# Scores of the last attention in three products of rounded parts, with two head groups on 64 rows each

## The chip, the cores and the metric

One core of a Trainium2 chip runs the whole program as one launch. The metric is the device time in microseconds. The clock of TensorE has two levels here, 1.2 and 2.4 GHz; the profile gives the granted clock of a stretch as a share of the upper one.

## The reference

Two model blocks over 512 tokens of width 1024, all in fp32. The first block has windowed attention with 12 heads, a retention branch and an MLP. The second has a short convolution layer and then an attention layer with three branches (`nsa_attention`): 16 query heads of width 64, 4 key and value groups. With 512 tokens and blocks of 64, all eight key blocks are selected, so the selected branch is a causal attention over all keys, and the window branch, window 512, is the same with other keys and values:

```
s_s = einsum(qr, kg) * scale;  p_s = masked_softmax(s_s);  o_s = p_s @ vg
s_w = einsum(qr, kw) * scale;  p_w = masked_softmax(s_w);  o_w = p_w @ vw
return g[..., 0:1] * o_c + g[..., 1:2] * o_s + g[..., 2:3] * o_w
```

The output of the attention is multiplied by silu(z), goes through one more projection, and the sum with the residual is normalized.

## The kernel before

Five engine programs are written from one list, `ORDER` (made by `make_order`). Each engine goes through this list and does its share of every token, strictly in the order of the list; semaphores carry the dependencies. `make_order` places tokens by tables of positions: `KV` for the projection stage of the last attention (a position is a step of TensorE's products), and for the attention itself one round per score unit, with `FILL` saying how many steps of other products (gate tiles `nz` 4 to 7, then the output projection `bo`) stand at three places of each round. The tables are written out as numbers in the file.

Almost all products are of the "rounded high and low" kind: an operand x is kept as a rounded copy h (type fp32r, ScalarE) and the remainder l = x - h (VectorE), and a product is h*h + h*l + l*h. This is how `mm` (L909), the retention (L998, L1009) and the values (L1141) work. The scores of the last attention (`scores_n`, L1115) are plain fp32 products instead.

The queries lie in `nqr[p]` (p is one of two pairs of key groups): partitions 0 to 63 are one group, 64 to 127 the other, each with four heads i. The keys lie in `ksT[:, n, p]` in the same way, n being the branch. There are 44 units `UNITS[u] = (p, qb, n, i0, cnt)`: a query block qb of 128 rows against N = (qb + 1) * 128 keys, for cnt heads in each of the two groups f. A unit takes two banks of a ring of three, one per f. The two groups' products read different 64 rows of the array. A bf16 product (L1118) adds the causal mask. Then, per unit: VectorE takes the maximum (L2140), ScalarE the exponential with its sum (L1161), GpSimd scales (L2230), TensorE turns the probabilities three rounds later (L1129, `LAG` = 3), ScalarE copies them rounded (L1536), VectorE takes the remainder (L2157), and TensorE makes the values (L1141). When a query block is complete, `gather` adds the halves (L1544, L2166), `gate_o` multiplies by silu(z) (L2178) and `split_o` makes high and low parts (L1560, L2184).

In the projection stage before it, keys and queries are projected and rotated (`rope_k`, `rope_q`, VectorE L2072, L2085), the compressed branch is computed (`cmp_scores`, `cmp_turn`, VectorE L2098 to L2126, ScalarE L1507), and weights are split (L1177 on ScalarE, L1636 on VectorE). Its last tokens are four `silu` on ScalarE; the first exponentials wait for the end of this stage on all engines.

Of the kernel before, what the change touches and what calls it, by code (L numbers as in the profile page):

```python
# [7 lines left out]
F32 = mybir.dt.float32  # L8
# [6 lines left out]
S = 512  # L15
# [294 lines left out]
def make_order():  # L310
# [83 lines left out]
    def some(n):  # L394
# [9 lines left out]
            out.append(pieces.pop(0))  # L404
        return out

    for r in range(len(UNITS) + LAG + 1):
        for G in GROUPS:
            if GROUPS[G][-1] == r - LAG - 1:
                if G == FIRST_GROUP[G[0], G[1]]:  # L410
                    o.append(("cmp_values", G[0], G[1]))
                o.append(("values_n", *G))
                if G == LAST_GROUP[G[0], G[1]]:
                    o.append(("gather", G[0], G[1]))
        o += some(FILL[r][0])
        if 0 <= r - LAG < len(UNITS):
            o.append(("turn_n", r - LAG))
        if 0 <= r - 1 < len(UNITS):
            o.append(("rate", r - 1))
        o += some(FILL[r][1])  # L420
        if r < len(UNITS):
            o.append(("scores_n", r))
        o += some(FILL[r][2])
        if r == SILU_AT:
            o += [("silu", f) for f in range(4, 8)]
        for G in GATED_AT:
            if GATED_AT[G] == r:
# [7 lines left out]
    for b in range(4):  # L435
# [4 lines left out]

LAG = 3

KV = {"k": 21, "v": 30, "gates": 23, "silu": 122, ("rope", 0, 0): 23, ("cmp", 0, 0): 43,
      ("turn", 0, 0): 64, ("rope", 0, 1): 36, ("cmp", 0, 1): 45, ("turn", 0, 1): 69, ("rope", 0, 2): 37,
      ("cmp", 0, 2): 52, ("turn", 0, 2): 75, ("rope", 0, 3): 41, ("cmp", 0, 3): 59, ("turn", 0, 3): 79,
      ("rope", 1, 0): 57, ("cmp", 1, 0): 82, ("turn", 1, 0): 95, ("rope", 1, 1): 67, ("cmp", 1, 1): 83,
# [10 lines left out]
SILU_AT = 22  # L457
GATED_AT = {(0, 0): 22, (0, 1): 24, (0, 2): 28, (0, 3): 38, (1, 0): 27, (1, 1): 32, (1, 2): 39}
ATT = {("norm", "q", 0, 0): 30, ("turn", "q", 0, 0): 51, ("norm", "q", 0, 1): 33, ("turn", "q", 0, 1): 54,
# [163 lines left out]
def program(nc, ctx, a, out):  # L623
# [77 lines left out]
        rs2 = sb("rs2", [128, S], F32, ph)  # L701
    ph3 = ExitStack()
    oT = sb("oT", [128, 8, S], F32, ph3)
    nqr = [sb(f"nqr{p}", [128, 4, S], F32, ph3) for p in range(2)]
    with ExitStack() as ph:
        nqu = [sb(f"nqu{p}", [128, 4, S], F32, ph) for p in range(2)]
    pcs = [sb(f"pc{p}", [128, 4, S], F32R, ph3) for p in range(2)]
    with ExitStack() as ph:
        cb = sb("cb", [128, 256], BF16, ph)
        cm = sb("cm", [128, 160], F32, ph)  # L710
        kcT = sb("kcT", [128, 2, 64], F32, ph)
        vc = sb("vc", [128, 4, 128], F32R, ph)
        ksT = sb("ksT", [128, 2, 2, S], F32, ph)
        v2 = sb("v2", [128, 4, 8, 128], F32R, ph)
        zx = sb("zx", [128, 2, S], F32, ph)
# [31 lines left out]
    Fb = [t[:, :, :].rearrange("p (a b) (c d) -> p a b c d", a=2, c=2) for t in (nqu[1], nqr[1])]  # L747

    XS = {"x": (xh, xl, "xl"), "or": (orh, orl, "orl"), "oa": (oah, oal, "oal"), "y": (yh, yl, "yl"),
          "h": (hh, hl, "hl"), "cy": (cyh, cyl, "cyl"), "z": (xh, xl, "zl")}  # L750
# [56 lines left out]
        return sl[(p * 4 + qb) % 2]  # L807

    def z_slot(f):
        return oT[:, 4 + f, :] if f < 4 else zx[:, f - 4, :] if f < 6 else tmp45[:, f - 6, :]  # L810

    def xo(b, c=None):

# [15 lines left out]
    def split_views(name, r, hi, lo):  # L829
# [20 lines left out]
    def tensor(e):  # L850
# [253 lines left out]
        def scores_n(u):  # L1104
            p, qb, n, i0, cnt = UNITS[u]
            qs = slice(qb * 128, qb * 128 + 128)
            N = (qb + 1) * 128
            two = [take("scores_n", ("scores_n", u, f), ("exp_n", u, f)) for f in range(2)]
            w.wait_ge(*told("cab"))
            w.wait_ge(*told("rope_done", "k", n, p))  # L1110
            for j in range(cnt):
                w.wait_ge(*told("rope_done", "q", p, i0 + j))
                for f, bank in enumerate(two):
                    hf = slice(64 * f, 64 * f + 64)
                    e.matmul(bank[:, j * N:(j + 1) * N], nqr[p][hf, i0 + j, qs], ksT[hf, n, p, 0:N], start=True,  # L1115
                             stop=False)
                for f, bank in enumerate(two):
                    m = e.matmul(bank[:, (j + 1) * N - 128:(j + 1) * N], idb, cab, start=False, stop=True)  # L1118
                    if j == cnt - 1:
                        m.then_inc(*tell("scores_n", u, f))  # L1120
# [33 lines left out]
    def scalar(e):  # L1154
# [348 lines left out]
        def cmp_turn(p, qb):  # L1503
# [78 lines left out]
        def end(phase):  # L1582
            S_.close(phase, "act")
            if phase == "att":
# [2 lines left out]

        follow(w_, w_part, w_piece, x_norm, x_in, x_raw, square, root, norm, v, rv, q, k_, norm_qk, turn_qk, scores, probs, values, mix_log, mix_pick, rq, rk,
               decay_parts, next_decay, rg, ret, gated_ret, ga, pb, split_oa, gb, pa, wo, up, down, z, ao, nsa_consts, fold, vsw, gate,
               hidden, compressed_v, nq_, cmp_scores, cmp_turn, scores_n, turn_n, gather, nz, silu, split_o,  # L1590
               final_gain, x_out, bo, bo_end, end)


    def vector(e):
# [413 lines left out]
        def key_in(n, p):  # L2008
# [15 lines left out]
        def rope_k(n, p):  # L2024
# [11 lines left out]
            e.tensor_tensor(ksT[:, n, p, :], ksT[:, n, p, :], t[:, :], ALU.add).then_inc(*tell("rope_done", "k", n, p))  # L2036

        def hidden(n):
            e.memset(hid[n][:, :, :, :, 31:32], 0.0).then_inc(*tell("hid_end", n))
# [29 lines left out]
        def nq_(p, i):  # L2069
            w.wait_ge(*told("out_a", ("nq", p, i)))  # L2070
            w.wait_ge(*told("cn"))
            e.tensor_tensor(nqr[p][:, i, :], nqu[p][:, i, :], cos, ALU.mult).then_inc(*tell("rope_cos", "q", p, i))  # L2072

        def rope_q(p, i):
            t = tmp[4 + p]
# [9 lines left out]
            e.tensor_tensor(nqr[p][:, i, :], nqr[p][:, i, :], t[:, :], ALU.add).then_inc(*tell("rope_done", "q", p, i))  # L2085

        def cmp_scores(p, qb):
            n = CMP.index((p, qb))
# [83 lines left out]
        def gate_o(p, qb):  # L2172
            c = slice(qb * 128, qb * 128 + 128)
            w.wait_ge(*told("silu", 4 * p + 3))
            w.wait_ge(*told("gathered", p, qb, 1))
            for k, z in ((4, zx), (6, tmp45)) if p else ((0, oT),):
                n = 2 if p else 4
                m = e.tensor_tensor(oT[:, k:k + n, c], oT[:, k:k + n, c], z[:, 0 if p else 4:2 if p else 8, c], ALU.mult)  # L2178
            m.then_inc(*tell("silu_mul", p, qb))

        def split_o(p, qb):
# [26 lines left out]
        def end(phase):  # L2208
# [1 line left out]

        follow(x_in, w_part, w_piece, x_norm, square, w_, root, norm, q, k_, norm_qk, turn_qk, scores, mix_log, mix_pick, mix, rq, rk, rv, decay, decay_parts, ret, gated_ret, pb, split_oa,
               gb, pa, wo, down, ao, up, c_, u, b_, z, nsa_consts, ck, cv, turn_rs, ks, kw, rope_k, hidden, compressed_k,
               compressed_v, gates, nq_, rope_q, vsw, cmp_scores, cmp_turn, scores_n, rate, turn_n, gather, gate_o,
               split_o, bo, bo_gain, bo_end, end)


# [133 lines left out]
```

## Time and profile before

| | us |
|---|---|
| median of three runs | 2043.85 |
| the three runs | 2041.2 to 2047.33 |
| span of the profiled execution | 2042.4 |
| projection stage of the last attention, from about | 1700 to 1795 |
| its attention rounds | 1795 to 2012 |

The page gives TensorE 98% of the span, VectorE 51%, ScalarE 38%, GpSimd 4%. The profile gives the time of its execution only as the span. In the rows below, PE is TensorE, PEld its weight loads, DVE VectorE, ACT ScalarE, POOL GpSimd. A busy time of PE covers the latency of a product too, so that products overlap in it; the distance of two starts is the pace.

### The profile page before, as it was taken

How to read it: one execution, taken by the hardware profiler on the slowest of the kernel's cores; microseconds unless marked ns; L12 is line 12 of the kernel's file. 1: busy time of each engine (PE TensorE's matmuls, PEld its weight loads, DVE VectorE, ACT ScalarE, POOL GpSimd, SP SyncE). 2: the span in 40 equal slices, each digit the busy share in tenths (PEclk: the TensorE clock that was granted, in tenths of full speed). 3: DMA queues.
4: the chain of work that ended last, by engine and by line, in shares of the span. 5: the costliest groups of instructions: out<-in, count | busy, mean ns of one | idle time of the engine just before them, and what ended most of it. 6: DMA issues, size and time to landing. Idle time of an engine off the chain costs nothing.

```text
span 2042.4 us, 22755 instructions
## 1 busy us (share of the span) xinstructions
PE 1996.0 (98%) x9502; PEld 1651.3 (81%) x9502; DVE 1051.4 (51%) x1415; ACT 771.5 (38%) x1232; POOL 80.6 (4%) x132
## 2 busy tenths in 40 slices
PE   7999999999999999999999999999999999999898
PEld 6899987888888888888888888888888788866566
DVE  4444447545454346643244455455454465856675
ACT  4554563342324323342143222212222214366764
POOL 0000000000000000000000000000000000033431
PEclk9999999999999999999999999999999999999999
DMA  5121222223232232233323332332333345210002
GB/s 206 63 83 62 83 83 67 88 88 97 74 103 66 100 103 83 91 97 102 103 89 97 103 100 86 103 103 83 103 103 83 119 124 152 80 42 22 32 21 63
DMA packets 186502, 181.25 MB, mean 89 GB/s; under 512 B 4896, under 2 KB 162976, under 8 KB 186400
## 3 DMA queue, kind: packets, MB, share of 16 engines
q1 hardware_dynamic: 182912, 172.41, 27.5%
q10 hardware_dynamic: 3488, 7.38, 1.3%
q8 instruction: 75, 1.23, 0.3%
q14 instruction: 27, 0.22, 0.0%
HBM read 173.49 MB, written 4.19 MB: 87 GB/s over the span
## 4 chain that ended last, share of the span: by engine, by line
PE 82%; DVE 9%; ACT 6%; issue 2%; DMA 1%; ACTq 0%; SPq 0%; DVEq 0%
PE bank L909 75%; ACT tmp L1161 2%; DVE tl L2157 2%; PE bank L1009 1%; DVE rs L2140 1%; ACT wh L1177 1%; PE bank L998 1%; ACT raw L1161 1%; PE bank L1141 1%; DVE wl L1636 1%; PE bank L1115 1%; DVE oT L2166 1%; ACT th L1536 0%; PE bank L919 0%; ACT pb L1161 0%
## 5 line engine op out<-in xcount | busy, mean ns | idle before, releaser
L909 PE MATMUL bank<-xh,wh 128*128 128x512 f32 x1352 | 534.7, 395 | 1.7 <-DVE wl L1636 1.1
L909 PE MATMUL bank<-xh,wl 128*128 128x512 f32 x1352 | 527.3, 390 | 0.0
L909 PE MATMUL bank<-xl,wh 128*128 128x512 f32 x1352 | 526.9, 390 | 0.0
L1636 DVE TENSOR_TENSOR wl<-raw,wh 128x2048 fp32r<-128x2048 f32 (+2 forms) x154 | 342.3, 2225 | 267.8 <-ACT wh L1177 267.5
L1177 ACT CAST wh<-raw 128x2048 fp32r<-128x2048 f32 (+2 forms) x154 | 285.2, 1854 | 382.3 <-PE bank L909 370.3
L909 PEld LDWEIGHTS bank<-xh,wh 128*128 128x128 f32 x1352 | 253.6, 188 | 55.4 <-issue 3.2
L909 PEld LDWEIGHTS bank<-xh,wl 128*128 128x128 f32 x1352 | 253.3, 187 | 54.2
L909 PEld LDWEIGHTS bank<-xl,wh 128*128 128x128 f32 x1352 | 253.7, 188 | 51.0 <-issue 0.7
L909 PE MATMUL bank<-wh,xh 128*128 128x512 f32 x512 | 213.5, 417 | 4.7 <-DVE xl L2184 4.0
L909 PE MATMUL bank<-wl,xh 128*128 128x512 f32 x512 | 202.0, 395 | 0.0
L909 PE MATMUL bank<-wh,xl 128*128 128x512 f32 x512 | 202.0, 395 | 0.0
L909 PEld LDWEIGHTS bank<-wh,xh 128*128 128x128 f32 x512 | 120.3, 235 | 17.1 <-issue 4.4
L909 PEld LDWEIGHTS bank<-wh,xl 128*128 128x128 f32 x512 | 120.1, 235 | 13.0
L909 PEld LDWEIGHTS bank<-wl,xh 128*128 128x128 f32 x512 | 121.2, 237 | 10.8
L2230 POOL TENSOR_SCALAR tmp<-tmp,rs 128x128 f32<-128x128 f32 (+3 forms) x88 | 54.4, 632 | 1884.7 <-DVE rs L2148 1884.7
L1161 ACT ACTIVATE tmp<-tmp 128x512 f32<-128x512 f32 (+2 forms) x61 | 36.6, 603 | 193.6 <-DVE tmp L1598 100.6
L909 PE MATMUL bank<-hh,wh 128*128 128x512 f32 x256 | 99.6, 389 | 0.0
L909 PE MATMUL bank<-hl,wh 128*128 128x512 f32 x256 | 99.6, 389 | 0.0
L909 PE MATMUL bank<-hh,wl 128*128 128x512 f32 x256 | 99.6, 389 | 0.0
L1885 DVE TENSOR_TENSOR xT<-xT,bank 128x512 f32<-128x512 f32 x32 | 22.0, 686 | 122.4 <-PE bank L909 122.4
L2157 DVE TENSOR_TENSOR tl<-bank,th 128x512 fp32r<-128x512 f32 (+1 forms) x88 | 52.4, 637 | 42.4 <-ACT th L1536 42.1
L1401 ACT CAST xh<-tmp 128x512 fp32r<-128x512 f32 x24 | 14.9, 621 | 150.0 <-DVE tmp L1894 150.0
(270 smaller groups left out, 2597.8 us busy)
## 6 DMA issues: line engine op xcount, KB each, us to landing
raw<-in_w_in SPq DMA_DIRECT2D x49, 1024.0 KB, 5.1
raw<-in_a_w_in SPq DMA_DIRECT2D x32, 1024.0 KB, 5.7
raw<-in_w_up SPq DMA_DIRECT2D x16, 1024.0 KB, 5.4
raw<-in_w_down SPq DMA_DIRECT2D x16, 1024.0 KB, 5.7
raw<-in_w_proj_b SPq DMA_DIRECT2D x8, 1024.0 KB, 5.1
raw<-in_a_w_out SPq DMA_DIRECT2D x8, 1024.0 KB, 5.6
raw<-in_w_out SPq DMA_DIRECT2D x4, 1024.0 KB, 5.0
raw<-in_w_kv SPq DMA_DIRECT2D x4, 1024.0 KB, 4.9
```

What stands on the lines that cost most here:

```text
L909: m = e.matmul(o, p, q, start=k == 0 and n == 0, stop=k == K - 1 and n == 2)
L998: m = e.matmul(bank[:, 0:n], k[:, kb * 128:(kb + 1) * 128], q[:, kb * 128:], start=j == 0 and x == 0, stop=j == 1 and x == 2)
L1009: m = e.matmul(bank[:, :], r[:, (qb - kb) * 128:(qb - kb + 1) * 128], v[:, kb, :], start=kb == 0 and x == 0, stop=kb == qb and x == 2)
L1115: e.matmul(bank[:, j * N:(j + 1) * N], nqr[p][hf, i0 + j, qs], ksT[hf, n, p, 0:N], start=True, stop=False)
L1141: m = e.matmul(bank_of("acc", (p, qb, f))[:, i0 * 128:(i0 + cnt) * 128], v2[:, k, n * 4 + p * 2 + f, :], t[:, 0:cnt * (qb + 1) * 128].rear ...
L1161: return e.activation(o, i, f, scale=scale, **kw)
L1177: m = e.copy(hi, r)
L1636: m = e.tensor_tensor(lo, r, hi, ALU.subtract)
L1885: e.tensor_tensor(xT[:, k, :], xT[:, k, :], tile_bank(key)[:, :], ALU.add).then_inc(*tell("out_d", key))
L2140: e.tensor_reduce(wt[:, c:c + cnt], bank_of("scores_n", ("scores_n", u, f))[:, 0:cnt * N].rearrange("p (s k) -> p s k", s=cnt), AX, ALU.ma ...
L2157: e.tensor_tensor(lo[:, o:o + m], bank_of("turn_n", ("turn_n", u, f))[:, 0:m], hi[:, o:o + m], ALU.subtract).then_inc(*tell("lo_n", u, f))
L2230: m = e.tensor_scalar(x, x, wt[:, 32 + c + j:33 + c + j], gts[:, qb, (p * 2 + f) * 4 + i0 + j, 1 + n:2 + n], ALU.mult, ALU.mult)
```

## The change

Queries and keys are first written in fp32 to `nqf` and `ksf` (the memory of `nqr` and `ksT`), and are then split: the rounded part by ScalarE, the remainder by VectorE, in place. Eight tokens `split_q` (512 columns each) and two `split_k` (1024 columns each) do this. `split_k` 0 stands at step 60 and `split_q` (0, 0) at the end of the projection stage, the others at the start of the rounds 0, 4, 12, 20, 22, 26, 34, and `split_k` 1 in round 20. `scores_n` makes three products for each head and group. To make room, the gate tiles 4 to 7 go to other memory, and wait for what was there.

```
+    extra += [(KV["split_k"], ("split_k", 0)), (KV["split_q"], ("split_q", 0, 0))]
...
+    splits = {r: [("split_q", p, qb)] for (p, qb), r in SPLIT_Q_AT.items()}
+    splits[SPLIT_K_AT].insert(0, ("split_k", 1))
     for r in range(len(UNITS) + LAG + 1):
+        o += splits.get(r, [])
...
+SPLIT_Q_AT = {(0, 1): 0, (0, 2): 4, (0, 3): 12, (1, 0): 20, (1, 1): 22, (1, 2): 26, (1, 3): 34}
+SPLIT_K_AT = 20
...
     def z_slot(f):
-        return oT[:, 4 + f, :] if f < 4 else zx[:, f - 4, :] if f < 6 else tmp45[:, f - 6, :]
+        return oT[:, 4 + f, :] if f < 4 else tmp45[:, 5 - f, :] if f < 6 else pcf[:, f - 6, :]
...
+            w.wait_ge(*told("split_lo", "k", p))
+            w.wait_ge(*told("split_lo", "q", p, qb))
+            qh, ql, kh, kl = q_hi(p, qb), nqr[p][:, :, qs], k_hi(p), ksT[:, :, p, :]
             for j in range(cnt):
-                w.wait_ge(*told("rope_done", "q", p, i0 + j))
-                for f, bank in enumerate(two):
-                    hf = slice(64 * f, 64 * f + 64)
-                    e.matmul(bank[:, j * N:(j + 1) * N], nqr[p][hf, i0 + j, qs], ksT[hf, n, p, 0:N], start=True,
-                             stop=False)
+                for x, (q, k) in enumerate(((qh, kh), (qh, kl), (ql, kh))):
+                    for f, bank in enumerate(two):
+                        hf = slice(64 * f, 64 * f + 64)
+                        e.matmul(bank[:, j * N:(j + 1) * N], q[hf, i0 + j, :], k[hf, n, 0:N], start=x == 0, stop=False)
...
+        def split_k(p):                     # ScalarE
+            w.wait_ge(*told("rope_done", "k", 1, p))
+            if p:
+                w.wait_ge(*told("cmp_pv", 0, 3))
+            else:
+                after("conv")
+            e.copy(k_hi(p), ksf[:, :, p, :]).then_inc(*tell("split_hi", "k", p))
+
+        def split_q(p, qb):                 # ScalarE
+            w.wait_ge(*told("rope_done", "q", p, 3))
+            if q_hi_before(p, qb):
+                w.wait_ge(*told("scores_n", LAST_UNIT[q_hi_before(p, qb)], 1))
+            elif qb:
+                w.wait_ge(*told("rope_done", "q", 1, 3))
+            e.copy(q_hi(p, qb), nqf[p][:, :, qb * 128:qb * 128 + 128]).then_inc(*tell("split_hi", "q", p, qb))
...
             after("kv" if f >= 4 else "conv")
+            if f == 5:
+                w.wait_ge(*told("scores_n", LAST_UNIT[0, 0], 1))
+            elif f > 5:
+                w.wait_ge(*told("cmp_pv", 0, f - 6))
...
+        def split_k(p):                     # VectorE
+            w.wait_ge(*told("split_hi", "k", p))
+            e.tensor_tensor(ksT[:, :, p, :], ksf[:, :, p, :], k_hi(p), ALU.subtract).then_inc(*tell("split_lo", "k", p))
+
+        def split_q(p, qb):                 # VectorE
+            c = slice(qb * 128, qb * 128 + 128)
+            w.wait_ge(*told("split_hi", "q", p, qb))
+            e.tensor_tensor(nqr[p][:, :, c], nqf[p][:, :, c], q_hi(p, qb), ALU.subtract).then_inc(*tell("split_lo", "q", p, qb))
...
-            for k, z in ((4, zx), (6, tmp45)) if p else ((0, oT),):
-                n = 2 if p else 4
+            for k, z in ((4, tmp45[:, 1:2, c]), (5, tmp45[:, 0:1, c]), (6, pcf[:, 0:2, c])) if p else ((0, oT[:, 4:8, c]),):
+                n = z.shape[1]
```

## Rows read from the trace of the kernel before

**Rows 1.** Busy us (and instructions) of each engine in two stretches, granted clock, DMA.
```profile
1742.00:1797.00 55.00, 53.30 (x285) 43.62 (x284) 47.15 (x99) 21.47 (x32) 0.00 (x0) 1.00 0.27 81
1795.00:2012.00 217.00, 197.63 (x1212) 138.43 (x1212) 138.06 (x283) 142.00 (x401) 80.39 (x128) 0.97 0.08 25
```
**Rows 2.** Chain of waits, 1876 to 1893 us: start, us, what.
```profile
1878.49 0.60 DVE rs L2140
1879.11 1.45 ACT tmp L1161 x4
1880.56 0.55 ACT th L1536
1881.13 1.29 DVE tl L2157 x2
...
1882.49 0.60 DVE rs L2140
```
**Rows 3.** Chain of waits from 1780 us on: shares by line, then pieces.
```profile
by line: DVE tl L2157 14.1%; ACT tmp L1161 12.6%; PE bank L909 11.1%; DVE rs L2140 7.8%; ACT raw L1161 5.7%; PE bank L1141 5.6%; PE bank L1115 5.4%; DVE oT L2166 4.7%; issue 4.7%; ACT th L1536 3.9%; PE bank L1129 2.9%; DVE xl L2184 1.9%; DM
...
1959.63 1.43 PE bank L1141 x12
...
1962.41 0.85 PE bank L1115 x4
...
1988.91 1.06 PE bank L1115 x4
```
**Rows 4.** Timeline of PE: start, us, instruction, count; score and mask products.
```profile
1795.14 0.49 PE L1115 MATMUL bank<-ksT,nqr 64*128 64x128 f32 x4
1795.56 0.28 PE L1118 MATMUL bank<-cb 128*128 128x128 bf16 x2
...
1941.03 0.59 PE L1115 MATMUL bank<-ksT,nqr 64*128 64x384 f32 x2
...
1941.45 0.49 PE L1115 MATMUL bank<-ksT,nqr 64*128 64x384 f32 x2
...
1941.87 0.28 PE L1118 MATMUL bank<-cb 128*128 128x128 bf16 x2
```
**Rows 5.** Timeline of PEld in the same unit: its second two loads.
```profile
1941.13 0.19 PEld L1115 LDWEIGHTS bank<-ksT,nqr 64*128 64x128 f32 x2
```
**Rows 6.** Timeline of PE: rounded products of the retention, 512 and 128 columns.
```profile
337.96 1.52 PE L998 MATMUL bank<-rqk 128*128 128x512 f32 x6
...
347.97 0.78 PE L998 MATMUL bank<-rqk 128*128 128x128 f32 x6
```
**Rows 7.** Timeline of ACT and DVE: two weight splits of 1024 columns.
```profile
1736.07 1.99 ACT L1177 CAST wh<-raw 128x1024 fp32r<-128x1024 f32 x2
...
1738.09 2.36 DVE L1636 TENSOR_TENSOR wl<-raw,wh 128x1024 fp32r<-128x1024 f32 x2 [1.20 <-ACT wh L1177]
```
**Rows 8.** Single lines: count, min/median/max ns, first and last start.
```profile
L1560 ACT CAST xh<-oT x8: 601/620/629, 1904.1 to 2014.3; 128x512 fp32r<-128x512 f32 x8
...
L2184 DVE TENSOR_TENSOR xl<-oT,xh x8: 692/692/820, 1904.8 to 2014.9; 128x512 fp32r<-128x512 f32 x8
```
**Rows 9.** Timeline of ACT, PE and DVE around the first scores; [idle before <-releaser].
```profile
1783.31 0.42 ACT L1161 ACTIVATE tmp<-tmp 128x256 f32<-128x256 f32 x1 [2.84 <-DVE tmp L2103]
...
1792.36 0.63 PE L1093 MATMUL bank<-base,tmp 128*64 128x128 f32 x4 [1.13 <-DVE pc L2126]
...
1796.02 2.19 ACT L1161 ACTIVATE oT<-oT 128x512 f32<-128x512 f32 x4
...
1796.58 0.69 DVE L2126 TENSOR_TENSOR pc<-bank,pc 64x512 fp32r<-64x512 f32 x1
...
1799.57 0.37 ACT L1161 ACTIVATE tmp<-bank,rs 128x128 f32<-128x128 f32 x1
```
**Rows 10.** Stretch as in rows 1, after the second score unit.
```profile
1806.20:1812.90 6.70, 6.70 (x27) 4.30 (x27) 2.10 (x4) 4.67 (x19) 3.57 (x9) 0.50 0.00 0
```
**Rows 11.** Timeline of PE: the scores of the third unit.
```profile
1806.16 1.22 PE L1115 MATMUL bank<-ksT,nqr 64*128 64x256 f32 x4 [1.61 <-ACT tmp L1161]
```

More of the change, by code:

```diff
@@ L441 @@
 LAG = 3
-KV = {"k": 21, "v": 30, "gates": 23, "silu": 122, ("rope", 0, 0): 23, ("cmp", 0, 0): 43,
+KV = {"split_k": 60, "split_q": 110, "k": 21, "v": 30, "gates": 23, "silu": 122, ("rope", 0, 0): 23, ("cmp", 0, 0): 43,
       ("turn", 0, 0): 64, ("rope", 0, 1): 36, ("cmp", 0, 1): 45, ("turn", 0, 1): 69, ("rope", 0, 2): 37,
@@ L703, in program @@
     oT = sb("oT", [128, 8, S], F32, ph3)
-    nqr = [sb(f"nqr{p}", [128, 4, S], F32, ph3) for p in range(2)]
+    with ExitStack() as ph:
+        nqf = [sb(f"nqf{p}", [128, 4, S], F32, ph) for p in range(2)]
+    nqr = [sb(f"nqr{p}", [128, 4, S], F32R, ph3) for p in range(2)]
     with ExitStack() as ph:
         nqu = [sb(f"nqu{p}", [128, 4, S], F32, ph) for p in range(2)]
+    with ExitStack() as ph:
+        pcf = sb("pcf", [128, 4, S], F32, ph)
     pcs = [sb(f"pc{p}", [128, 4, S], F32R, ph3) for p in range(2)]
@@ L712, in program @@
         vc = sb("vc", [128, 4, 128], F32R, ph)
-        ksT = sb("ksT", [128, 2, 2, S], F32, ph)
+        with ExitStack() as ph2:
+            ksf = sb("ksf", [128, 2, 2, S], F32, ph2)
+        ksT = sb("ksT", [128, 2, 2, S], F32R, ph)
         v2 = sb("v2", [128, 4, 8, 128], F32R, ph)
-        zx = sb("zx", [128, 2, S], F32, ph)
+        kh0 = sb("kh0", [128, 2, S], F32R, ph)
         with ExitStack() as ph2:
@@ L746, in program @@
     Ab = nqu[0][:, :, :].rearrange("p (a b) (c d) -> p a b c d", a=2, c=2)
-    Fb = [t[:, :, :].rearrange("p (a b) (c d) -> p a b c d", a=2, c=2) for t in (nqu[1], nqr[1])]
+    Fb = [t[:, :, :].rearrange("p (a b) (c d) -> p a b c d", a=2, c=2) for t in (nqu[1], nqf[1])]
     XS = {"x": (xh, xl, "xl"), "or": (orh, orl, "orl"), "oa": (oah, oal, "oal"), "y": (yh, yl, "yl"),
@@ L809, in z_slot, with q_hi, q_hi_before, k_hi @@
     def z_slot(f):
-        return oT[:, 4 + f, :] if f < 4 else zx[:, f - 4, :] if f < 6 else tmp45[:, f - 6, :]
+        return oT[:, 4 + f, :] if f < 4 else tmp45[:, 5 - f, :] if f < 6 else pcf[:, f - 6, :]
+    def q_hi(p, qb):
+        if (p, qb) == (0, 0):
+            return rsl1[:, 0, :].rearrange("p (i q) -> p i q", i=4)
+        if (p, qb) == (0, 1):
+            return th2[:, S:2 * S].rearrange("p (i q) -> p i q", i=4)
+        if qb >= 2:
+            return nqr[p][:, :, (qb - 2) * 128:(qb - 1) * 128]
+        return nqr[0][:, :, 0:128] if qb else nqr[0][:, :, 256:384]
+    def q_hi_before(p, qb):
+        return {(0, 2): (0, 0), (0, 3): (0, 1), (1, 0): (0, 2), (1, 1): (0, 2), (1, 2): (1, 0), (1, 3): (1, 1)}.get((p, qb))
+    def k_hi(p):
+        return pcs[0][:, 2:4, :] if p else kh0[:, :, :]
     def xo(b, c=None):
@@ L837, in split_views @@
         return [(r, hi, lo)]
+    LAST_UNIT = {(x[0], x[1]): u for u, x in enumerate(UNITS)}
     LAST_P0 = max(u for u, x in enumerate(UNITS) if x[0] == 0)
@@ L1109, in scores_n @@
             w.wait_ge(*told("cab"))
-            w.wait_ge(*told("rope_done", "k", n, p))
+            w.wait_ge(*told("split_lo", "k", p))
+            w.wait_ge(*told("split_lo", "q", p, qb))
+            qh, ql, kh, kl = q_hi(p, qb), nqr[p][:, :, qs], k_hi(p), ksT[:, :, p, :]
             for j in range(cnt):
-                w.wait_ge(*told("rope_done", "q", p, i0 + j))
-                for f, bank in enumerate(two):
-                    hf = slice(64 * f, 64 * f + 64)
-                    e.matmul(bank[:, j * N:(j + 1) * N], nqr[p][hf, i0 + j, qs], ksT[hf, n, p, 0:N], start=True,
-                             stop=False)
+                for x, (q, k) in enumerate(((qh, kh), (qh, kl), (ql, kh))):
+                    for f, bank in enumerate(two):
+                        hf = slice(64 * f, 64 * f + 64)
+                        e.matmul(bank[:, j * N:(j + 1) * N], q[hf, i0 + j, :], k[hf, n, 0:N], start=x == 0, stop=False)
                 for f, bank in enumerate(two):
@@ L1589, in scalar @@
                decay_parts, next_decay, rg, ret, gated_ret, ga, pb, split_oa, gb, pa, wo, up, down, z, ao, nsa_consts, fold, vsw, gate,
-               hidden, compressed_v, nq_, cmp_scores, cmp_turn, scores_n, turn_n, gather, nz, silu, split_o,
+               hidden, compressed_v, nq_, cmp_scores, cmp_turn, split_k, split_q, scores_n, turn_n, gather, nz, silu, split_o,
                final_gain, x_out, bo, bo_end, end)
@@ L2015, in key_in @@
             w.wait_ge(*told("cn"))
-            e.tensor_tensor(ksT[:, n, p, :], t[:, :], cos, ALU.mult).then_inc(*tell("rope_cos", "k", n, p))
+            e.tensor_tensor(ksf[:, n, p, :], t[:, :], cos, ALU.mult).then_inc(*tell("rope_cos", "k", n, p))
         def ks(p):
@@ L2035, in rope_k @@
             w.wait_ge(*told("rope_cos", "k", n, p))
-            e.tensor_tensor(ksT[:, n, p, :], ksT[:, n, p, :], t[:, :], ALU.add).then_inc(*tell("rope_done", "k", n, p))
+            e.tensor_tensor(ksf[:, n, p, :], ksf[:, n, p, :], t[:, :], ALU.add).then_inc(*tell("rope_done", "k", n, p))
         def hidden(n):
@@ L2071, in nq_ @@
             w.wait_ge(*told("cn"))
-            e.tensor_tensor(nqr[p][:, i, :], nqu[p][:, i, :], cos, ALU.mult).then_inc(*tell("rope_cos", "q", p, i))
+            e.tensor_tensor(nqf[p][:, i, :], nqu[p][:, i, :], cos, ALU.mult).then_inc(*tell("rope_cos", "q", p, i))
         def rope_q(p, i):
@@ L2084, in rope_q @@
             w.wait_ge(*told("rope_cos", "q", p, i))
-            e.tensor_tensor(nqr[p][:, i, :], nqr[p][:, i, :], t[:, :], ALU.add).then_inc(*tell("rope_done", "q", p, i))
+            e.tensor_tensor(nqf[p][:, i, :], nqf[p][:, i, :], t[:, :], ALU.add).then_inc(*tell("rope_done", "q", p, i))
         def cmp_scores(p, qb):
@@ L2175, in gate_o @@
             w.wait_ge(*told("gathered", p, qb, 1))
-            for k, z in ((4, zx), (6, tmp45)) if p else ((0, oT),):
-                n = 2 if p else 4
-                m = e.tensor_tensor(oT[:, k:k + n, c], oT[:, k:k + n, c], z[:, 0 if p else 4:2 if p else 8, c], ALU.mult)
+            for k, z in ((4, tmp45[:, 1:2, c]), (5, tmp45[:, 0:1, c]), (6, pcf[:, 0:2, c])) if p else ((0, oT[:, 4:8, c]),):
+                n = z.shape[1]
+                m = e.tensor_tensor(oT[:, k:k + n, c], oT[:, k:k + n, c], z, ALU.mult)
             m.then_inc(*tell("silu_mul", p, qb))
@@ L2212, in vector @@
                gb, pa, wo, down, ao, up, c_, u, b_, z, nsa_consts, ck, cv, turn_rs, ks, kw, rope_k, hidden, compressed_k,
-               compressed_v, gates, nq_, rope_q, vsw, cmp_scores, cmp_turn, scores_n, rate, turn_n, gather, gate_o,
+               compressed_v, gates, nq_, rope_q, vsw, cmp_scores, cmp_turn, split_k, split_q, scores_n, rate, turn_n, gather, gate_o,
                split_o, bo, bo_gain, bo_end, end)
```

## The prediction

> **What bounds the kernel now.** I read the page's busy times first, then the stretches, then the chain of waits, then single instructions. The page gives TensorE 98% of the span, which says nothing about the last attention alone. The stretches do: from 1795 to 2012 us TensorE is busy 197.6 of 217 us, VectorE 138.1, ScalarE 142.0 [rows 1]. So nobody is full, and a wait must be found. The chain of waits shows two kinds of bound. In most rounds it never touches TensorE: the maximum of a score tile (VectorE L2140, 0.60), two exponentials (ScalarE L1161, 1.45), the first rounded copy of an older turned tile (ScalarE L1536, 0.55), two remainders of it (VectorE L2157, 1.29), a reciprocal, and the next maximum, 4.00 us later [rows 2]. Each engine works its list in order, so VectorE and ScalarE wait for each other in a ring, and TensorE fits beside it. In other rounds filler products and score products are on the chain: L1141, L909, and then the scores of round 35 at 1962.41 [rows 3]. The reader should see that these are different resources: a shorter score product helps only in the second kind, and one more instruction on ScalarE or VectorE hurts in the first.
>
> **What the score products cost now.** One head pair (j) with 384 keys: two matmuls start together at 1941.03, one for each half of the rows; the next two at 1941.45; the mask product at 1941.87 [rows 4]. The second loads are issued at 1941.13 [rows 5]. I read this as 0.105 us for a load that nothing covers, two passes of 0.32 us over 384 columns (2 cycles a column at 2.4 GHz), and 0.10 us until the mask product. The same formula gives 0.42 for 128 columns (rows: 1795.14 to 1795.56), 0.845 for 384 (0.85), and 1.06 for 512 (1.06) [rows 3, 4], so 0.635 for 256 is safe. The pairs therefore already overlap in fp32; that the heads sit on 64 rows each is not new.
>
> **What they cost after.** Three rounded passes instead of two fp32 passes. A rounded pass is one column a cycle: six products of 512 columns take 1.52 with a last one of 0.389, so 0.226 apart [rows 6]; twelve of 256 columns take 1.43, 0.119 apart [rows 3]; I put 384 between at 0.175. For 128 columns the six take 0.78 with a last one of about 0.22, so 0.112 apart [rows 6]: the weight load sets the pace there, not the 0.053 of streaming. No row shows two rounded products on 64 rows each side by side; I take it that they overlap as the fp32 ones do. For one j:
> - 128 columns: 0.105 + 2 x 0.112 + 0.055 + 0.10 = 0.49, against 0.42: 0.07 more
> - 256: 0.105 + 3 x 0.119 + 0.10 = 0.56, against 0.635: 0.07 less
> - 384: 0.73, against 0.845: 0.11 less
> - 512: 0.885, against 1.06: 0.175 less
>
> There are 16 j of each size, so TensorE is given back 16 x 0.285 = 4.6 us. If no pair overlapped the passes would double, and a j would take 0.83, 0.92, 1.26, 1.56: 26 us more. The bounds are -4.6 and +26; I take the first, since the same two half arrays overlap in the rows. All j together take 16 x (0.42 + 0.635 + 0.85 + 1.06) = 47 us now, and the chain from 1780 us to the end (262 us) has 5.4% on L1115, 14 us [rows 3]; so I count 14 x 4.6 / 47, -1.4, on the path.
>
> Here a rule bears on the sum. The pairs start 0.42 apart in two fp32 passes and each pass is fully shared [rows 4]. The Trainium skill (TensorE: Matmul & The Clock Gate, Part 3: Packing small matmuls) states that products on different row groups run side by side, but gives 3.07 times for four of them. By that factor a shared pass would be 1.3 times as long, a j of 512 columns an estimated 1.09 instead of 0.885, and the 4.6 us would be gone. Nothing else below uses this.
>
> **What is added.** Eight copies of a 128x512 piece of the queries (ScalarE) and eight subtractions (VectorE), two each of 128x1024 for the keys. Nearest rows: 1.99 for two and 2.36 for two of 128x1024, so 1.0 and 1.18 [rows 7]; 0.62 and 0.69 for 128x512 [rows 8]. By order:
> - split_k(0), step 60 of the projection stage. VectorE is busy 47.2 of 55 us there [rows 1], and its idle gaps are waits for a ScalarE exponential that itself had waited 2.84 us for VectorE [rows 9]. So the two go in lockstep from about 1758 on. TensorE waits at the end for VectorE: 1.13 us at 1792.36 [rows 9]. The 1.0 of the copy runs beside; the 1.18 of the subtraction moves the end. +1.2.
> - split_q(0,0) at the last step and split_q(0,1) at the start of round 0. ScalarE runs four Silu from 1796.02, a table load, and the first exponential at 1799.57 [rows 9], with no gap between. Two copies go in. VectorE ends the projection stage with the remainder at 1796.58 [rows 9], and now has two subtractions before the first maximum; the second waits for its copy, behind the Silu. And the first score product waits for split_q(0,0): 1797.27 + 1.2 + 0.69 = 1799.15 instead of 1795.14. Four j of 0.49 and three masks of 0.22 end at 1801.8, the maximum takes 0.6, so the first exponential starts at 1802.7: +3.1, of which +1.2 is the line above. +1.9. The second score unit is again 128 columns: +0.2 (its four j lie on the path).
> - Rounds 4, 12, 26: one split_q each, between the exponentials of one round and the rounded copy of the next. ScalarE gives up 0.5 to 0.6, then subtraction (0.62 from start to start) and L1536 (0.55) run side by side. +0.67 each, +2.0. All three rounds are ring rounds like [rows 2].
> - Round 20: split_k(1) and split_q(1,0). Copy 1.0, then subtraction 1.15 and subtraction 0.62 against 0.55 of L1536 that they cover: +2.2. This is the ring of [rows 2] itself.
> - Round 22: before four Silu and two table loads on ScalarE: +0.65.
> - Round 34: the copy delays a ring in a TensorE stretch; round 35's scores wait for TensorE until 1962.41 [rows 3], and the delayed exponential would be ready at 1961.7. Nothing, or 0.67 if that cover goes.
> - gate_o for the second half: three multiplications instead of two, +0.05 to +0.1 each: +0.2. The gate tiles' new slots add waits for the scores of unit 1 and for cmp_values, both long done when nz 5, 6 and 7 land: nothing. The SP queue and its transfers are not moved.
>
> Every other new wait looks two rounds ahead (a block's pieces are split two rounds before its first scores) and costs nothing; behind the first score product 12 filler products are queued, and they had 3 us of slack.
>
> **The sum.** 1.2 + 1.9 + 0.2 + 2.0 + 2.2 + 0.65 + 0.2 - 1.4 = +7.0 us. The profile gives its execution by the span of 2042.4 alone; that is 1.4 under the median of 2043.85 and inside the three runs (2041.2 to 2047.33). Profiled span after: 2049.4; on the median: 2050.8. Each added piece counts 0 if TensorE covers it and its full copy plus subtraction if nothing overlaps, so the additions lie between 1.9 and 14.
>
> **Rivals.**
> - A, TensorE is the engine that decides (91% busy in the stage): the additions of the rounds fall in the 75 us that ScalarE is idle, and all 4.6 are on the path. For it: the stretches of [rows 3]. Against: the ring of [rows 2], with TensorE waiting at every second round. 1.2 + 1.9 - 4.6 = -1.5; if the half-speed stretch from 1806 to 1813 (granted clock 0.50 [rows 10]) goes too, about -4: 2040 to 2042. It decides as soon as ScalarE and VectorE have over 0.7 us spare in the rounds named.
> - B, half the additions are hidden and the gain on the path is 2.5: +2.5, 2046.5.
> - C, the clock. TensorE now idles 3 us before the first scores. In the profile the stretch at the lower level, 1.2 GHz [rows 10], begins with an idle time of 1.61 us before 1806.16 [rows 11]. If it comes at once, the four j take twice as long, +2.6, and the later one may stay: 2053.5.
> - D, rounded pairs do not overlap: +26 us of TensorE against 19 us of idle time in the stage, of which about half can take it up: 2043.85 + 3 + 15 = 2062.
>
> **How the numbers follow.** My forecast (+7.0) 0.42, A 0.12, B 0.22, C 0.16, D 0.08. The range must take in B and C and half of A: 2043 to 2057. A measurement of this kernel tells about 0.3% (6.1 us) from no change: faster means under 2037.7, slower over 2050.0. The forecast lies just beyond that edge: of it 0.55 is slower, with C and D, so 0.47; faster needs more than A and gets 0.06; the rest, 0.47, is within.
>
> **What would show it.** A j of 512 columns from first score to mask 0.88 (if 1.06 or more, the pass rule is wrong; if 1.5, D). Pairs of matmuls 6 ns apart, three times. First scores at 1799 and first exponential at 1802.7. The maximum of round 20 about 2.2 us later against that of round 19 than now (4.0 between them), TensorE idle in it. Distance from the first maximum of round 34 to that of 35 shorter by 0.6. If the distance between rounds 4, 12 and 26 and those before does not grow, the ring is not what bounds, and A is right.

## The result, and the profile after

| | before | after |
|---|---|---|
| median us (4 runs each) | 2043.09 | 2057.22 |
| lowest to highest | 2041.2 to 2047.33 | 2054.96 to 2058.73 |
| span of the profiled execution | 2042.4 | 2054.5 |

The ratio is 1.0067, 95% interval 1.0056 to 1.0079: slower by 0.67%, and clear of noise, since the interval lies well above 1. The forecast was 2050.8, range 2043 to 2057: right in direction, too small by 6.4 us, and the time lies 0.2 us above the range. The two spans differ by 12.1 us, and the rest of this section accounts for those.

The busy times of the same two stretches (columns as in [rows 1]) seem to say the opposite of the result. In the second, TensorE is busy 188.0 us instead of 197.6, VectorE and ScalarE about as long as before. But the rounds now end 12 us later, so that the same 217 us hold less of their work: the figures don't mean that TensorE was given back 10 us.

```profile
1742.00:1797.00 55.00, 52.24 (x263) 42.53 (x261) 47.16 (x99) 21.76 (x32) 0.00 (x0) 0.97 0.26 80
1795.00:2012.00 217.00, 188.01 (x1274) 141.64 (x1274) 137.66 (x283) 140.20 (x396) 76.45 (x125) 0.96 0.07 23
```

**The score products.** Timeline of PE in the changed kernel, one j of 512 columns (start, us, instruction, count). From the first score product to the mask it takes 0.89 us.

```profile
1989.23 0.50 PE L1147 MATMUL bank<-pc,nqr 64*128 64x512 f32 x2
1989.57 0.39 PE L1147 MATMUL bank<-ksT,nqr 64*128 64x512 f32 x2
1989.80 0.39 PE L1147 MATMUL bank<-pc,nqr 64*128 64x512 f32 x2
1990.12 0.28 PE L1149 MATMUL bank<-cb 128*128 128x128 bf16 x2
```

The reader should see "x2" three times: the two head groups start together, and the third pair follows the second by 0.23, one pass of 512 columns. Over all rounds the median j takes 0.48, 0.56, 0.73 and 0.89 for the four sizes, forecast 0.49, 0.56, 0.73 and 0.885. In the kernel before the medians were 0.42, 0.635, 0.85 and 1.06, so TensorE is given back 5.0 us (forecast 4.6). Shared passes are not longer than single ones here. The Trainium skill (TensorE: Matmul & The Clock Gate, Part 3: Packing small matmuls) gives 3.07 times for four products; the prediction's estimate from it, passes 1.3 times as long, is not seen for two.

**The start.** Timelines of PE, DVE and ACT around the first unit; in brackets the idle time before, and what ended it.

```profile
1797.87 0.69 DVE L2187 TENSOR_TENSOR nqr<-nqf,rsl 128x512 fp32r<-128x512 f32 x1
...
1798.71 0.33 PE L1147 MATMUL bank<-kh,rsl 64*128 64x128 f32 x2 [1.65 <-DVE nqr L2187]
...
1801.97 1.29 DVE L2200 TENSOR_REDUCE rs<-bank 128x4 f32<-128x512 f32 x2 [1.43 <-PE bank L1149]
...
1802.69 0.37 ACT L1192 ACTIVATE tmp<-bank,rs 128x128 f32<-128x128 f32 x1 [1.58 <-DVE rs L2200]
```

TensorE waits for the remainder of block (0, 0) and starts at 1798.71 (forecast 1799.15); the first exponential starts at 1802.69 (forecast 1802.7), 3.1 us after that of [rows 9]. This execution was already 0.52 us ahead of that of before at 1688, ahead of everything that was changed; so the delay that the change makes is 3.6 us, not the 3.1 of the forecast. `split_k` 0 is 1.1 of it (forecast 1.2): the first maximum of the compressed scores behind it (L2101, then L2152) is at 1775.99 instead of 1775.41, in a list that ran 0.52 ahead.

**Round 20.** Chain of waits of the changed kernel: start, us, what. This is the ring of [rows 2] with two splits in it.

```profile
1886.94 0.60 DVE rs L2200
1887.54 0.03 issue
1887.57 1.45 ACT tmp L1192 x4
1889.01 0.94 ACT pc L1546
1889.96 0.03 issue
1889.98 1.23 DVE ksT L2182
1891.21 0.60 DVE nqr L2187
1891.81 0.61 DVE tl L2217
1892.42 0.04 issue
1892.47 3.40 PE bank L1172 x16
```

The copy L1546 and the subtractions L2182 and L2187 add 0.94 + 1.23 + 0.60; the rounded copy (0.55) that stood there in [rows 2] has gone under them: 2.2. What follows was not forecast: the 16 value products take 3.40, 0.21 apart, because the clock is down.

**The clock.** Six stretches of the changed kernel (columns as in [rows 1]; the granted clock is the third number from the end).

```profile
1793.98:1797.39 3.41, 2.93 (x6) 1.82 (x6) 2.62 (x3) 3.38 (x5) 0.00 (x0) 0.50 0.00 0
1800.80:1804.21 3.41, 3.41 (x16) 2.81 (x15) 1.29 (x2) 1.83 (x10) 0.00 (x0) 0.50 0.24 90
1892.96:1896.37 3.41, 3.41 (x19) 3.41 (x18) 1.30 (x4) 1.45 (x4) 1.52 (x2) 0.50 0.00 0
1995.37:1998.77 3.40, 3.40 (x17) 3.40 (x18) 1.68 (x4) 1.45 (x4) 1.52 (x2) 0.50 0.51 154
...
1789.98:1793.40 3.42, 1.23 (x8) 0.65 (x6) 2.77 (x8) 3.21 (x7) 0.00 (x0) 1.00 0.91 304
1806.20:1812.90 6.70, 5.14 (x51) 3.50 (x49) 1.29 (x2) 2.77 (x17) 3.19 (x8) 1.00 0.00 0
```

In the first four TensorE is granted 0.50 (1.2 GHz) while it has work. Before the first of them it was busy 1.23 of 3.42 us; before the third it idled 2.80 us, until 1892.47. The last line is the stretch of [rows 10], which ran at 0.50 in the kernel before and runs at 1.00 here. The clock is also at 0.50 from 1913.44 to 1920.27, where the account below shows no loss; the kernel before has two such stretches, from 1905.13 and from 1929.02.

**The whole account.** For each round I take the start of its first maximum (L2140 before, L2200 after) and subtract: a ladder of shifts, whose steps show where time arises. They add up to the spans' difference.

| step | forecast | measured |
|---|---|---|
| projection stage, first unit, second unit | +3.3 | +3.56, then +2.07 in round 1, then -2.17 in rounds 2 and 3, where the slow stretch of before is absent: +3.46 |
| rounds 4, 12, 26 | +2.0 | 0.60 + 0.74 + 0.64 = +1.98 |
| round 20 | +2.2 | +2.20 |
| round 21 | 0 | +1.55 (clock 0.50) |
| round 22 | +0.65 | +0.60 |
| rounds 24, 25 (gate_o) | +0.2 | +0.33 |
| rounds 34, 35 | 0 | +0.74, -0.30: +0.44 |
| round 41 | 0 | +1.36 (clock 0.50) |
| TensorE's gain | -1.4 | 0.10 + 0.11 + 0.17 + 0.18: -0.56 |
| after the last round, and rest | 0 | +0.71 |
| sum | +7.0 | +12.07 |

The -2.17 in the first line is not the change's doing. A kernel with the scores and splits of before (slots alone, below) was profiled at a span of 2039.7 us, 2.7 under that of before, and it wins the same in rounds 2 and 3, -1.22 and -0.75: its clock doesn't fall there (columns as in [rows 1], now of that kernel).

```profile
1806.20:1812.90 6.70, 6.67 (x44) 4.31 (x44) 3.97 (x8) 4.42 (x18) 4.45 (x10) 1.00 0.00 0
```

So the profiled execution of before happened to hold a slow stretch worth about 2 us. The start costs 5.6 us rather than 3.46, and that is about what the ladder's 12.1 lacks against the 14.1 of the medians.

### The profile page after: what moved, and what is told of

The parts are those of the page before. It is cut to its first block, busy times and chain, and to the rows that moved or that the text cites. A ratio compares the mean times of both kernels' runs of the same rounds, so it can differ in the third digit from the quotient of the medians.

```text
span 2054.5 us, 23037 instructions
## 1 busy us (share of the span) xinstructions
PE 1995.4 (97%) x9630; PEld 1662.5 (81%) x9630; DVE 1058.2 (52%) x1429; ACT 777.0 (38%) x1242; POOL 79.9 (4%) x132
## 4 chain that ended last, share of the span: by engine, by line
PE 81%; DVE 10%; ACT 6%; issue 2%; DMA 1%; ACTq 0%; SPq 0%; DVEq 0%
PE bank L939 73%; ACT tmp L1192 2%; DVE tl L2217 2%; PE bank L1039 1%; DVE wl L1687 1%; ACT wh L1208 1%; DVE rs L2200 1%; PE bank L1172 1%; PE bank L1028 1%; ACT raw L1192 1%; DVE oT L2226 1%; PE bank L1147 1%; PE bank L949 0%; PE bank L1160 0%; ACT pb L1192 0%
```

## Experiments

My theory: ScalarE and VectorE, one after the other, set the time of most rounds, so that each split costs what it adds to this ring, and the score products' time hardly counts. Rivals: TensorE decides; the new slots cost something; the lower clock carries most of it. Shifts below are against the profiled execution of before. Up to 1688 us, where nothing is changed, profiled executions differ by -1.45 to +0.54 us; small ends of the ladders carry this. Medians are given beside those of the kernel before on the same chip.

### The parts one at a time

**Splits without the products.** All splits are done, and the scores stay fp32.

```
-                for x, (q, k) in enumerate(((qh, kh), (qh, kl), (ql, kh))):
+                for f, bank in enumerate(two):
+                    e.matmul(bank[...], nqf[p][hf, i0 + j, qs], ksf[hf, n, p, 0:N], start=True, stop=False)
```

> The scores stay plain fp32 products, as before, but all ten splits (ScalarE copy, VectorE subtraction) are done where the change puts them, their results unused, and the gate tiles are in their new slots. Theory (the splits lie in the ring of ScalarE and VectorE): nearly all of the change's loss is here, +3 at the first scores, +0.6 to 0.75 at each of the rounds 4, 12, 22, 26, +2.2 at round 20; with stretches at the lower clock 9 to 13 us over the kernel before. Rival 1 (the loss is TensorE's: three passes, six weight loads, a lower clock from their shortness): at most +4. Rival 2 (the gate tiles' slots and waits): as much as the change, and the slots alone as well.

Measured: 2056.22 against 2042.18, ratio 1.0066 (1.0052 to 1.0079): the whole loss. The first maximum is at +4.83, more than the 3 I expected, and round 1 adds +2.93 (clock 0.50 from 1801.1 to 1807.9). The steps are +0.60 in round 4, +0.74 in 12, +2.19 in 20, +2.15 in 21 (clock 0.50 from 1893.2 to 1900.1), +0.60 in 22, +0.63 in 26.

**Products without the splits.** Three products of the same rounded operands; the low parts are left out.

```
-                for x, (q, k) in enumerate(((qh, kh), (qh, kl), (ql, kh))):
+                for x, (q, k) in enumerate(((qh, kh), (qh, kh), (qh, kh))):
```

> No splits at all: queries and keys are rounded as they are rotated, and the scores make three products of these same rounded operands (the low parts are left out; TensorE does the work of the change). Gate tiles in their new slots. Theory: -1 to -2.5 us against the kernel before, since a unit's scores are 0.1 to 0.17 us shorter per pair and few of them are on the path; the shift ladder by rounds stays within 1 us, other than by clock. Rival 1 (TensorE's part costs): +5 or more.

Measured: 2045.01 against 2042.18, 1.0013 (1.0004 to 1.0022): 2.8 us slower, where I had expected 1 to 2.5 faster. The profiled span is 2041.4, 1.0 under that of before, but this comes from rounds 1 to 3 (+0.51, -1.37, -0.13), where the execution of before had its slow stretch. Behind them there are -0.10 to -0.17 in rounds 11, 13, 15 and 41, +0.42 in round 33 and +0.11 in round 35, which cancel. So the 5 us taken from TensorE give back nothing, and the median even loses a little. The granted clock over the whole span is 0.994 in the median of these runs and 0.996 in those of before; that the clock takes the 2.8 us is likely but not shown.

**Slots alone.** fp32 scores, no splits, only the gate tiles' new places.

```
+        return oT[:, 4 + f, :] if f < 4 else tmp45[:, 5 - f, :] if f < 6 else pcf[:, f - 6, :]
...
+            if f > 5:
+                w.wait_ge(*told("cmp_pv", 0, f - 6))
```

> The kernel before with gate tiles 4 to 7 in the new slots, and gate_o for the second half in three multiplications instead of two; nothing else. Theory: +0.2 us, no difference to be seen. Rival 2 (slots and their waits cost): +3 or more.

Measured: 2042.26, 1.0002 (0.9993 to 1.0011). The slots cost nothing. (The changed kernel's wait of gate tile 5 for the scores of unit 1 is not in this run.)

**One product instead of three.** The two products with low parts are left out, the splits stay.

```
-                for x, (q, k) in enumerate(((qh, kh), (qh, kl), (ql, kh))):
+                for x, (q, k) in enumerate(((qh, kh),)):
```

> The changed kernel with only the product of the two rounded high parts; the two products with the low parts are left out, all splits stay. TensorE loses two passes of every j: 2 x 0.11, 0.119, 0.175 and 0.228 for the four sizes, 16 x 1.26 = 20.3 us. Ring theory (ScalarE and VectorE set most rounds, TensorE's score time is on the path for 14 of 47 us): of the first 4.6 us given back 1.0 reached the end, so of these 20.3 some 4 to 6 do, 2051 to 2053, and the steps of rounds 4, 12, 20, 22, 26 stay as they are (0.6, 0.7, 2.2, 0.6, 0.6). Rival (TensorE decides in the stage): 2037, and the steps at the splits vanish. Third: the longer idle times of TensorE bring more stretches at the lower clock and the gain is under 3 us.

Measured: 2056.92 against 2042.28, 1.0069 (1.0056 to 1.0082), the same as with three. The median j takes 0.26, 0.32, 0.37 and 0.43: against the changed kernel 16 x 1.28, 20.5 us of TensorE are gone, and no time. The stretch of the rounds in this kernel, columns as in [rows 1]:

```profile
1795.00:2012.00 217.00, 177.94 (x1023) 130.58 (x1022) 138.21 (x284) 141.90 (x397) 76.46 (x125) 0.91 0.07 23
```

TensorE is busy 177.9 us instead of 188.0, and the mean clock falls from 0.96 to 0.91. Its ladder gains 0.47 in round 11 and 0.65 in round 35, and loses +1.08 in round 4 and +0.92 in round 15 (the clock is at 0.50 from 1811.4 to 1821.7 and from 1866.1 to 1869.5); round 41 loses 1.06. My expected 4 to 6 us failed, the third case is what came: the gain is under 3 us. The lower clock alone doesn't explain why nothing is gained: in rounds 5 to 10 and 16 to 19 the shift against the kernel before moves by no more than 0.03 us, with three products, with one, and with the fp32 scores. And the steps stay, 0.74 in round 12, 2.19 in 20, 0.60 in 22, 0.63 in 26 and 0.74 in 34. This settles for the rounds the rival that TensorE decides.

### The splits on another engine

GpSimd is busy 80 of 217 us in the rounds. There the copy of 128x512 takes 0.61, the subtraction 1.28 (in the runs below).

**Eight of the ten splits on GpSimd.** `split_k` 0 and `split_q` (0, 0) stay.

```
+        def split_q(p, qb):                 # GpSimd; ScalarE and VectorE only for (0, 0)
...
+            e.tensor_copy(q_hi(p, qb), nqf[p][:, :, c])...
...
+            e.tensor_tensor(nqr[p][:, :, c], nqf[p][:, :, c], q_hi(p, qb), ALU.subtract)...
```

> The change, but the seven split_q from round 0 on and split_k 1 are done whole by GpSimd (copy and subtraction), which is idle two thirds of these rounds; split_k 0 and split_q (0, 0) stay on ScalarE and VectorE. Theory: the insertions in the ring go (-5 to -6 us), half of the start's +1.9 too, and round 20's low clock with its idle time; the time is 0 to +4 us against the kernel before. If GpSimd's pieces take over 3 us each and rate waits behind them, a wait for the turned tiles comes instead (+1 to +3 more). Rival 1 (TensorE's part costs): as slow as the change, +12 to +14.

Measured: 2050.95 against 2042.18, 1.0037 (1.0024 to 1.0049): +8.8, more than the 0 to +4 that I expected. The steps of rounds 4, 12 and 20 are gone, rounds 22 and 26 keep 0.31 and 0.22. But the start is as late as in the changed kernel: the first maximum is at +2.92, which is 4.2 against this execution's place at 1688, where the changed kernel has 4.1. The copy and subtraction of block (0, 1) thus cost nothing there; what costs is `split_k` 0 and `split_q` (0, 0). Round 21 still gives +1.56 at clock 0.50.

**All ten on GpSimd.** `KP` and `QP` list the splits of keys and queries that GpSimd does.

```
+KP = (0, 1)
+QP = ((0, 0), (0, 1), (0, 2), (0, 3), (1, 0), (1, 1), (1, 2), (1, 3))
```

> The change with all ten splits on GpSimd, those of the projection stage too, where it has nothing else to do. Theory: with the start's insertions gone as well as the ring's, only TensorE's shorter scores are left: the first maximum where it was (within 0.5 us), no step at the rounds with a split, -1 us at the end as in the run with the products only; 0 to +3 in the median, with what the lower clock takes. Rival (GpSimd beside VectorE slows VectorE, or TensorE's part costs): +5 or more.

Measured: 2046.8 against 2042.51, 1.0023 (1.0014 to 1.0032): +4.3, between my 0 to +3 and the rival's +5. Two steps are left: the first maximum comes 1.1 late after the 0.5 that is there at 1688, and round 22 gives +1.06.

**Only the three splits of the start on GpSimd.**

```
+KP = (0,)
+QP = ((0, 0), (0, 1))
```

> The complement of the run with the late splits on GpSimd: here split_k 0 and split_q (0, 0) and (0, 1) are GpSimd's, the other seven stay on ScalarE and VectorE. Theory: the two parts add up; the shift at the first maximum (3.6 us in the changed kernel) goes, with the low clock there, and the steps at rounds 4, 12, 20, 22, 26, 34 stay; +8 to +10 over the kernel before. Rival (one place is the cause and the rest follows from it): as the kernel before, or as the change.

Measured: 2052.8 against 2042.51, 1.0056 (1.0042 to 1.007): +10.3. The first maximum is at +1.66, and the steps of rounds 4 (0.64), 12 (0.74), 20 (2.20), 22 (0.60), 26 (0.64) and 34 (0.74) are back; round 21 gives +2.30 at clock 0.50. Start and rounds thus add up almost as the ladder says.

**Why the start stayed 1.1 late.** The timelines of POOL and DVE in the kernel with all splits on GpSimd:

```profile
1743.51 0.42 DVE L2160 TENSOR_REDUCE rs<-tmp 128x8 f32<-128x256 f32 x1
...
1743.77 1.29 POOL L2334 TENSOR_TENSOR nqr<-nqf,rsl 128x512 fp32r<-128x512 f32 x1
...
1743.96 1.39 DVE L2162 TENSOR_TENSOR tmp<-tmp,rs 128x256 f32<-128x256 f32 x1
```

L2162 usually takes 0.42; here it takes 1.39 and ends 0.29 after GpSimd's subtraction (1745.06). The same line takes 0.65 beside the second subtraction, and the first L1701 of round 22 takes 1.75 instead of 0.67 beside the one at 1893.81. All of these read both operands from SBUF. L2229 and L2212, with an operand in PSUM, keep their times beside such subtractions. The Trainium skill has this rule (SBUF — State Buffer, Who interferes with whom): a VectorE instruction with two SBUF inputs contends with a GpSimd instruction that reads SBUF, and the port pair that they share is an exclusive lock. The trace agrees: all three end 0.27 to 0.55 us after GpSimd's subtraction. So I moved the three splits concerned.

```
+            if (p, qb) == (0, 0):
+                w.wait_ge(*told("cmp_probs", 1, 3))
+            if (p, qb) == (0, 1):
+                w.wait_ge(*told("nmx_n", 0, 1))
-SPLIT_Q_AT = {..., (1, 1): 22, ...}
+SPLIT_Q_AT = {..., (1, 1): 23, ...}
```

> All splits on GpSimd as in the run where it had all ten, but the three whose subtraction met a VectorE instruction with two operands in SBUF are moved: block (0,0) waits for the last compressed probabilities, block (0,1) for the first maxima, block (1,1) goes to round 23. In the earlier run VectorE's L2162 took 1.39 instead of 0.42 beside the first subtraction, 0.65 beside the second, and L1701 1.75 instead of 0.67 beside the one of round 22. Blocking theory (VectorE stands still until GpSimd's subtraction ends): the first maximum comes 1.1 earlier, the 1.06 of round 22 goes, in all 1.5 to 2.2 less than 2046.8: 2044.6 to 2045.3, no longer told from the kernel before. Rival (the 1.1 belongs to the new waits or slots, the 1.06 to the lower clock there): 2046 to 2047.

Measured: 2043.37 against 2042.28, ratio 1.0006 (0.9997 to 1.0015): not told from the kernel before, and 1.2 better than I expected. POOL and DVE in this kernel, L2162 back at 0.42 and the pair of L1701 at 1.29 (2.35 where it was blocked):

```profile
1743.10 0.42 DVE L2162 TENSOR_TENSOR tmp<-tmp,rs 128x256 f32<-128x256 f32 x1
...
1791.99 1.28 POOL L2338 TENSOR_TENSOR nqr<-nqf,rsl 128x512 fp32r<-128x512 f32 x1
...
1892.63 1.29 DVE L1701 TENSOR_TENSOR wl<-raw,wh 128x512 fp32r<-128x512 f32 x2 [1.91 <-ACT wh L1218]
```

The first maximum is at -0.42, of which -0.32 is there at 1688; round 22 gives 0.00. The blocking theory holds for both. The span is 2041.3. With every split out of the ring the change costs nothing that can be told from noise, and it gains nothing either.

### The lower clock

**Filler before the first scores.** The filler steps of round 0 stand ahead of its scores, so that TensorE doesn't wait.

```
-FILL = [(1, 1, 4), ...
+FILL = [(3, 3, 0), ...
```

> The change, with the six filler steps of round 0 all ahead of the first scores (before: two ahead, four behind). TensorE then works instead of waiting for split_q (0, 0). Theory: no idle time before the first scores, which then run at the upper clock (0.48 a pair instead of 0.84); 1 to 2.5 us faster than the change, so +11 to +13 over the kernel before. Rival (the clock's fall there is not from the idle time): no difference to the change.

Measured: 2054.56 against 2042.51, 1.0063 (1.0049 to 1.0076): +12.1. The idle time before the first scores falls from 1.65 to 0.18 and the whole first unit runs at the upper clock; but there are 1.52 us of idle time before the second unit's scores, and the clock is 0.50 from 1805.8 to 1816.0 instead, in rounds 1 and 2 (a j of 0.84 and 0.94), and by round 3 the shift is 3.1 instead of 3.5. The stretch was moved, not removed.

**Filler in round 20.** Three steps from rounds 15 and 17.

```
-FILL: 15 (0, 1, 1), 17 (1, 1, 0), 20 (0, 0, 0)
+FILL: 15 (0, 0, 0), 17 (1, 0, 0), 20 (1, 1, 1)
```

> The change, with three filler steps taken from rounds 15 and 17 and put into round 20, where TensorE idles 0.9 and 2.8 us while ScalarE and VectorE split. Theory (the step of 1.55 us at round 21 is the lower clock that this idle time brings): the step goes, TensorE's clock stays at the upper level in rounds 20 to 22; 1 to 2 us faster than the change. Rival (the step is split_q (1, 0)'s own wait): it stays, or the fillers lengthen round 20.

Measured: 2056.16 against 2042.51, 1.0063 (1.005 to 1.0075). TensorE's idle time falls from 2.80 to 1.79, and round 21 still gives +1.47, at 0.50 from 1892.0 to 1895.4. Missed.

**The two splits of round 20 apart.**

```
-SPLIT_Q_AT = {..., (1, 0): 20, ...}
+SPLIT_Q_AT = {..., (1, 0): 21, ...}
```

> The changed kernel with the split of block (1,0) in round 21 instead of 20, where that of the second keys stays. The first maxima of rounds 20 and 21 are now 2.2 and 1.5 later than before. If the unforeseen 1.5 is the lower clock that follows TensorE's idle time of 2.8 us: the idle time is cut in two, the clock stays up, round 20 gives 1.55, round 21 0.65, 1.5 us less in all: 2055.7. Rival (the lower clock comes anyway, from what TensorE does over the whole of rounds 19 to 21, or the second step is the queue's own): the sum of both stays 3.7, 2057.

Measured: 2054.88 against 2042.28, 1.0059 (1.0047 to 1.0072). Round 20 gives +1.60 as expected, round 21 +1.43 instead of 0.65, at 0.50 from 1894.7 to 1898.1; both sum to 3.0 instead of 3.75. TensorE's longest idle time before it is 2.19 instead of 2.80. The kernel with the splits cleared off the ring has the same step, +1.54 in round 21, with no idle time above 0.91 us in the twenty microseconds before. Its stretch at the lower clock and the one ahead of it:

```profile
1883.80:1887.20 3.40, 3.40 (x18) 3.40 (x17) 1.38 (x4) 1.45 (x4) 3.32 (x4) 0.50 0.00 0
1880.38:1883.79 3.41, 1.91 (x14) 1.14 (x13) 2.02 (x4) 2.41 (x6) 3.32 (x5) 1.00 0.00 0
```

TensorE had been busy 1.91 of 3.41 us there. So the long idle time that the splits make is not needed for the clock to fall in that round, and my explanation of the 1.55 by it is not shown. What the runs show is that rounds 19 to 22 are a place where the clock often falls: it did in the changed kernel and in the others above, though in the products alone (from 1894.2), the slots alone (from 1900.2) and all ten on GpSimd (from 1895.8) only behind round 21. What picks the moment stays open.

## Why the prediction was right, and where it was short

- **The ring bounds the rounds**: shown. In the rounds each split cost what it adds to ScalarE, then VectorE, less what goes under it. Rounds 4, 12, 26 and 20 were forecast at 2.0 and 2.2 and came at 1.98 and 2.20; on GpSimd these steps vanish; without the products they stay.
- **The products**: each size of j right within 0.01. Rival D (26 us) is out.
- **TensorE's gain, -1.4**: mis-sized. I took a share of the chain of waits [rows 3] for what a shorter product would save. Only four steps, 0.56 together, were left; the products alone made the median 2.8 slower, and even 20.5 us less gained nothing. Rival A had an end of 2040 to 2042.
- **The start, +3.3**: 3.46 net, which is luck. The work of the start came at 5.6, and the 2.17 taken off again belong to the slow stretch in the profiled execution of before. The first exponential was right to 0.01 us, but from an execution that ran 0.52 ahead. The +0.2 for the second unit was too small: round 1 gives about 0.5 in four other kernels with the new scores, at the upper clock. Rival C said the clock would fall at once, with all four j of the first unit at twice the time, +2.6. It did fall, at 1793.98 and at 1800.80, but between the two it was at 1.00, and only the last j (0.83 from 1800.81 to 1801.64) was slow. Round 1 lost 2.07, and most of it is this clock. So C named the right mechanism at the start, though not its timing.
- **Round 34**: forecast nothing with its cover. The cover was 0.7 less than thought: +0.74, of which TensorE's stretch gave back 0.30.
- **What was missing**: the two later stretches at 0.50, 1.55 in round 21 and 1.36 in round 41, are 2.9 of the 5.1 us; TensorE's gain is 0.84, round 34 is 0.44, and 0.71 behind the last rounds was not followed up. The prediction took up the clock only at the start. The further 2 us between the difference of the spans (12.1) and that of the medians (14.1) match the slow stretch in the profiled execution of before.
- **Two sums of the prediction don't come out of its own terms.** All copies and subtractions together are 14.8, not 14. In B, half of the additions less 2.5 is 8.35 / 2 - 2.5 = +1.7, not +2.5. Neither moves the forecast.

## What to carry to other kernels

Before making an operation cheaper, look for what the chain of waits does around it: where two other engines hand each other the work, a faster product gains nothing, and each instruction added to those two costs its full time less what it overlaps. If such an instruction must be added, put it on the engine that is not in the ring, and at a place where it meets no VectorE instruction with two operands in SBUF. And look at the granted clock of more than one execution before explaining a step of 2 us: here a stretch at the lower clock cost 0.9 to 2.9 us in the rounds where it met the chain of waits and nothing in others, it came and went between executions of the same work, and three attempts to avoid it moved it at best.

## What the runs showed of the hardware

- Two rounded products on 64 rows each overlap fully: pairs of 512 columns start 0.23 apart, as single ones do. The fp32 pairs overlap too: both products of a pair start at once [rows 4].
- A rounded product of 128 columns is 0.11 apart from the next, in pairs as alone; so three passes of it (0.48 a j) are slower than two in fp32 (0.42).
- GpSimd copies 128x512 to a rounded type in 0.61 us, as fast as ScalarE (0.62), and subtracts in 1.28, against VectorE's 0.69.
- A VectorE subtraction with both operands in SBUF stood still until GpSimd's was done: 1.39 and 1.75 us instead of 0.42 and 0.67.
- TensorE's clock fell to 0.50 in one kernel though no idle time had been above 0.91 us in the twenty microseconds before; it had been busy for 1.91 of the last 3.41 us.
- With nearly equal work the clock fell in one execution (1806 to 1813, kernel before) and not in another (slots alone).
